# Expert stage of a two-layer decoder trunk: last strip's gate and up weights side by side, one-hot matrix transposed on another engine, activations' parts in the tokens' tile

## What is computed

```python
def swiglu(h, w_gate, w_up, w_down):
    return (jax.nn.silu(h @ w_gate) * (h @ w_up)) @ w_down

def moe_ffn(h, w_router, w_gate, w_up, w_down):       # hf: 256 x 1024
    logits = (hf @ w_router).astype(jnp.float32)
    top_vals, top_idx = lax.top_k(logits, TOP_K)      # TOP_K = 2 of 8
    top_w = jax.nn.softmax(top_vals, axis=-1)
    ...
    for e in range(N_EXPERTS):
        out = out + gates[:, e:e + 1].astype(hf.dtype) * swiglu(hf, w_gate[e], w_up[e], w_down[e])
```

## Time and profile before

| | |
|---|---|
| median of three runs | 1274.0 us (1270.16 to 1275.53) |
| profiled execution | 1273.91 us, span 1272.1 us |
| PE busy | 1231.5 us (97%) |
| DVE busy | 996.6 us (78%) |
| ACT busy | 831.1 us (65%) |
| POOL busy | 87.1 us (7%) |
| moved from and to HBM | 282 GB/s over the span |
| first expert item begins | about 485 us |
| last matmul of the last item begins | 1259.6 us |

### The profile page before, as it was taken

One profiled execution on the slowest core, in us unless ns is written; L12 is line 12 of the kernel. 1 busy time (PEld: TensorE's weight loads), 2 busy tenths in 40 slices (PEclk: granted clock), 3 DMA queues, 4 the chain that ended last, 5 costly groups with the idle time before them and its releaser, 6 DMA issues.

```text
span 1272.1 us, 17697 instructions
## 1 busy us (share of the span) xinstructions
PE 1231.5 (97%) x6322; PEld 1027.1 (81%) x6322; DVE 996.6 (78%) x1156; ACT 831.1 (65%) x919; POOL 87.1 (7%) x71
## 2 busy tenths in 40 slices
PE   8998999999999898999999999999999999999997
PEld 8976788888897576888888888888888888888775
DVE  4785566655668748898888888888888888888996
ACT  5556554454554746777777777777777777777764
POOL 2000000000000002010010010010010010010830
PEclk8988999999999899999999999999999999999999
DMA  9430665555452039999999999999999999999961
GB/s 295 153 132 2 205 226 178 188 175 193 121 182 101 16 105 398 394 387 375 392 366 369 391 363 362 392 366 375 391 363 369 392 362 370 392 364 369 396 224 50
DMA packets 186373, 357.54 MB, mean 281 GB/s; under 512 B 15255, under 2 KB 73173, under 8 KB 186292
## 3 DMA queue, kind: packets, MB, share of 16 engines
q1 hardware_dynamic: 183436, 344.89, 75.8%
q0 software_dynamic: 2688, 11.46, 2.4%
q10 hardware_dynamic: 200, 0.54, 0.1%
HBM read 351.11 MB, written 7.86 MB: 282 GB/s over the span
## 4 chain that ended last, share of the span: by engine, by line
PE 88%; DVE 6%; ACT 3%; issue 2%; DMA 1%; POOL 0%; SPq 0%; POOLq 0%; DVEq 0%; ACTq 0%
PE bank L1610 23%; PE bank L1612 23%; PE bank L1611 23%; PE bank L1911 6%; PE bank L1912 3%; PE bank L1979 1%; DVE lo_ring L1108 1%; PE bank L1689 1%; ACT hi_ring L766 1%; PE bank L1794 1%; DMA raw_a<-in_w_in 1%; DMA raw_a<-in_w_gate_dense 1%; PE bank L1960 1%; DVE lo_ring L1103 1%; DVE cv L1214 1%
## 5 line engine op out<-in xcount | busy, mean ns | idle before, releaser
L1108 DVE TENSOR_TENSOR lo_ring<-raw_m,hi_ring 128x2048 fp32r<-128x2048 f32 x168 | 389.6, 2328 | 53.4 <-ACT hi_ring L772 52.5
L772 ACT ACTIVATE hi_ring<-raw_m 128x2048 fp32r<-128x2048 f32 x168 | 322.2, 1918 | 80.0 <-PE bank L1612 80.0
L1610 PE MATMUL bank<-hi_ring,hT 128*128 128x512 f32 (+1 forms) x832 | 318.7, 383 | 3.2 <-DVE lo_ring L1108 3.0
L1612 PE MATMUL bank<-hi_ring,hT 128*128 128x512 f32 (+1 forms) x832 | 311.7, 375 | 0.0
L1611 PE MATMUL bank<-lo_ring,hT 128*128 128x512 f32 (+1 forms) x832 | 311.0, 374 | 0.0
L1108 DVE TENSOR_TENSOR lo_ring<-raw_a,hi_ring 128x2048 fp32r<-128x2048 f32 x96 | 220.8, 2310 | 35.9 <-ACT hi_ring L772 35.7
L772 ACT ACTIVATE hi_ring<-raw_a 128x2048 fp32r<-128x2048 f32 x96 | 183.4, 1920 | 53.5 <-PE bank L1612 52.3
L1610 PEld LDWEIGHTS bank<-hi_ring,hT 128*128 128x128 f32 x832 | 157.2, 189 | 33.7 <-DVE lo_ring L1108 6.9
L1103 DVE TENSOR_TENSOR lo_ring<-raw_a,hi_ring 128x2048 fp32r<-128x2048 f32 (+1 forms) x55 | 124.2, 2262 | 71.5 <-ACT hi_ring L766 71.4
L1612 PEld LDWEIGHTS bank<-hi_ring,hT 128*128 128x128 f32 x832 | 156.8, 188 | 28.8
L1611 PEld LDWEIGHTS bank<-lo_ring,hT 128*128 128x128 f32 x832 | 157.3, 189 | 26.4
(11 more groups left out here) (317 smaller groups left out, 1507.0 us busy)
## 6 DMA issues: line engine op xcount, KB each, us to landing
raw_m<-in_w_down_exp SPq DMA_DIRECT2D x80, 1024.0 KB, 7.0
raw_a<-in_w_up_exp SPq DMA_DIRECT2D x48, 1024.0 KB, 6.8
raw_m<-in_w_gate_exp SPq DMA_DIRECT2D x48, 1024.0 KB, 7.6
raw_a<-in_w_gate_exp SPq DMA_DIRECT2D x40, 1024.0 KB, 6.9
raw_m<-in_w_up_exp SPq DMA_DIRECT2D x40, 1024.0 KB, 7.9
raw_a<-in_w_in SPq DMA_DIRECT2D x12, 1024.0 KB, 6.4
raw_a<-in_w_gate_dense SPq DMA_DIRECT2D x11, 1024.0 KB, 5.4
raw_a<-in_w_up_dense SPq DMA_DIRECT2D x11, 1024.0 KB, 5.4
```

Of the source, the lines that this page charges most:

```text
L772: A(hi_of(NA + j), t, ACT.Copy).then_inc(hi_ready, 1)
L1108: V.tensor_tensor(lo_of(NA + j), expert_slot(i, j)[0], hi_of(NA + j).bitcast(F32), ALU.subtract).then_inc(lo_ready, 1)
L1610: M(o, lh, rh, start=start, stop=False)
L1612: return M(o, ll, rh, start=False, stop=stop)
```

## The change

Three things. (1) `m_hi` and `m_lo` are no tiles of their own any more but views of `y_hi` and `y_lo`, in the second half of `hT`. (2) The last strip's gate and up weights are put side by side: two pieces "GU", each with four blocks of 128 rows, 256 gate columns and 256 up columns, loaded by two transfers each. One matmul of 512 columns computes both into bank 0; Silu reads its left half and the product its right half. The list has 33 pieces as before and ends with GU, GU, D4, D4, D5. (3) TensorE's transposes of `onehot` and ScalarE's copies go. Instead VectorE keeps, per item, the slots' token numbers: the second column of the token table is raised by one, so that a slot without a token is told apart, and at U4 VectorE copies `tok_next` to `tok_now` and writes the next item's numbers from bank 7. After the last item it compares them with `iota` to make `onehot_t` once; `scatter` waits for that. VectorE's wait for the transposes ahead of `make_onehot` goes too.

```diff
@@ expert_order
     order = up("G", 0) + up("U", 0)
-    for c in range(1, EC):
+    for c in range(1, EC - 1):
         order += up("G", c) + up("U", c) + down(c - 1)
-    return order + down(EC - 1)
+    return order + [("GU", EC - 1, part) for part in range(2)] + down(EC - 2) + down(EC - 1)
@@ tables
-        one[:, K_TOK + 2 * t:K_TOK + 2 * t + 2] = (t * P + np.arange(P))[:, None]
+        one[:, K_TOK + 2 * t] = t * P + np.arange(P)
+        one[:, K_TOK + 2 * t + 1] = t * P + np.arange(P) + 1.0
@@ tiles
+        tok_now = sb("tok_now", [P, TT])
+        tok_next = sb("tok_next", [P, TT])
-        m_hi = sb("m_hi", [P, 2, 4, P], F32R)
-        m_lo = sb("m_lo", [P, 2, 4, P], F32R)
+        m_hi = y_hi.rearrange("p (c f s) -> p c f s", c=2, f=4)
+        m_lo = y_lo.rearrange("p (c f s) -> p c f s", c=2, f=4)
@@ helpers
+        def closes(kind, c, part, which):
+            return kind in (which, "GU") and last_part(kind, c, part)
+        def up_out(which, c):
+            if c < EC - 1:
+                return bank["GU".index(which)][:, 0:EW]
+            return bank[0][:, FC * "GU".index(which):FC * "GU".index(which) + FC]
         def transposed_after(kind, c, part):
-            if kind == "G" and c >= 1 and last_part(kind, c, part):
+            if kind == "G" and c >= 1 and last_part(kind, c, part) or kind == "GU" and part == 0:
                 return c - 1
@@ sync, expert_loads
+                    elif kind == "GU":
+                        rows = PIECE // EW * P
+                        for m, name in enumerate(("w_gate_exp", "w_up_exp")):
+                            src = a[name][0][one, part * rows:(part + 1) * rows, c * EW:c * EW + FC
+                                             ].rearrange("e (k p) n -> p (e k) n", p=P)
+                            sp.dma_start(expert_view(t, kind, c)[:, :, m * FC:(m + 1) * FC], src).then_inc(s, 16)
+                        continue
@@ scalar, item
-                    if kind == "G" and last_part(kind, c, part):
+                    if closes(kind, c, part, "G"):
                         act.wait_ge(piece_used, expert_done(i, "G", c))
                         act.wait_ge(prod_done, GU0 + c + i * EC)
-                        A(m_sg[:, 0:w], bank[0][:, 0:w], ACT.Silu).then_inc(sg_done, 1)
-                    if kind == "U" and c == 2 and part == 0:
-                        act.wait_ge(onehot_tmm, i + 1)
-                        A(onehot_t[:], bank[6][:, 0:TT * P].rearrange("p (t s) -> p t s", t=TT),
-                          ACT.Copy).then_inc(onehot_tdone, 1)
+                        A(m_sg[:, 0:w], up_out("G", c), ACT.Silu).then_inc(sg_done, 1)
@@ vector, item
-                    if kind == "U" and last_part(kind, c, part):
+                    if closes(kind, c, part, "U"):
-                        V.tensor_tensor(m_prod[:, 0:w], bank[1][:, 0:w], m_sg[:, 0:w], ALU.mult).then_inc(prod_done, 1)
+                        V.tensor_tensor(m_prod[:, 0:w], up_out("U", c), m_sg[:, 0:w], ALU.mult).then_inc(prod_done, 1)
                     if kind == "D" and c == 2 and part == 0:
-                        dve.wait_ge(onehot_tmm, i + 1)
+                        if first:
+                            dve.wait_ge(gather_mm, 4)
                     if kind == "U" and c == 4 and part == 0:
+                        if first:
+                            V.memset(tok_now[:], 0.0).then_inc(tok_moved, 1)
+                        else:
+                            dve.wait_ge(tok_kept, TT * i)
+                            V.tensor_copy(tok_now[:], tok_next[:]).then_inc(tok_moved, 1)
                         dve.wait_ge(slot_mm, i + 1)
                         V.tensor_copy(slot_i[:], bank[7][:, 0:1]).then_inc(slot_ready, 1)
+                        dve.wait_ge(tok_moved, i + 1)
+                        for t in range(TT):
+                            V.tensor_scalar(tok_next[:, t:t + 1], bank[7][:, 1:2], -1.0 - t * P, None, ALU.add
+                                            ).then_inc(tok_kept, 1)
@@ vector, after the last item
+            dve.wait_ge(tok_moved, n_items)
+            for t in range(TT):
+                V.tensor_scalar(onehot_t[:, t, :], iota, tok_now[:, t:t + 1], None, ALU.is_equal).then_inc(onehot_tdone, 1)
@@ tensor, scatter
+                    pe.wait_ge(onehot_tdone, TT)
@@ tensor, item
-                            pe.wait_ge(onehot_tdone, i + 1)
-                            if kind == "G":
+                            if kind != "U":
                                 pe.wait_ge(sg_done, GU0 + c + i * EC)
-                        o = bank[0 if kind == "G" else 1][:, 0:w]
-                        for kk in range(PIECE // w):
-                            k = part * (PIECE // w) + kk
+                        o = bank[1 if kind == "U" else 0][:]
+                        for kk in range(PIECE // EW):
+                            k = part * (PIECE // EW) + kk
-                    if kind == "U" and c == 2 and part == 0:
-                        for t in range(TT):
-                            r = nc.tensor.transpose(bank[6][:, t * P:(t + 1) * P], onehot[:, t, :].bitcast(F32), ident)
-                        r.then_inc(onehot_tmm, 1)
```

More of the change, by code:

```diff
@@ L445, in build @@
         gathered = sem("gathered")
-        onehot_tmm = sem("onehot_tmm")
+        tok_kept = sem("tok_kept")
+        tok_moved = sem("tok_moved")
         onehot_tdone = sem("onehot_tdone")
@@ L488, in expert_slot @@
             tile = raw_a[:, s, :] if s < RAW_A else raw_m[:, s - RAW_A, :]
-            return tile, raw_in[s], 16 * (trunk_uses[s] + j // RAW_M + 1) + i * (16 * NFF // RAW_M)
+            sent = [2 if E_ORDER[m % NFF][0] == "GU" else 1 for m in range(s, 2 * NFF, RAW_M)]
+            return tile, raw_in[s], 16 * (trunk_uses[s] + sum(sent[0:j // RAW_M + 1])) + i * (16 * sum(sent[0:NFF // RAW_M]))
         def in_piece_view(t, p):
@@ L514, in last_part @@
         def last_part(kind, c, part):
-            return part == expert_width(c) // FC - 1
+            return part == (2 if kind == "GU" else expert_width(c) // FC) - 1
         def expert_done(i, kind, c):
-            return NA + E_ORDER.index((kind, c, expert_width(c) // FC - 1)) + 1 + i * NFF
+            kind = "GU" if kind != "D" and c == EC - 1 else kind
+            parts = 2 if kind == "GU" else expert_width(c) // FC
+            return NA + E_ORDER.index((kind, c, parts - 1)) + 1 + i * NFF
         def expert_view(t, kind, c):
-            return t.rearrange("p (k n) -> p k n", n=D if kind == "D" else expert_width(c))
+            return t.rearrange("p (k n) -> p k n", n=D if kind == "D" else EW)
+        def closes(kind, c, part, which):
[4 more added lines that the diff above has]
+            return bank[0][:, FC * "GU".index(which):FC * "GU".index(which) + FC]
         def transposed_after(kind, c, part):
-            if kind == "G" and c >= 1 and last_part(kind, c, part):
+            if kind == "G" and c >= 1 and last_part(kind, c, part) or kind == "GU" and part == 0:
                 return c - 1
@@ L606, in expert_loads @@
                         src = a["w_down_exp"][0][one, f0:f0 + FC, :].rearrange("e (k p) n -> p (e k) n", p=P)
+                    elif kind == "GU":
[5 more added lines that the diff above has]
+                        continue
                     else:
                         w = a["w_gate_exp" if kind == "G" else "w_up_exp"][0]
-                        rows = PIECE // expert_width(c) * P
-                        src = w[one, part * rows:(part + 1) * rows, c * EW:c * EW + expert_width(c)
+                        rows = PIECE // EW * P
+                        src = w[one, part * rows:(part + 1) * rows, c * EW:(c + 1) * EW
                                 ].rearrange("e (k p) n -> p (e k) n", p=P)
@@ L1984, in item @@
                     pe.wait_ge(lo_ready, NR + j + 1 + i * NFF)
-                    w = expert_width(c)
                     wh, wl = expert_view(hi_of(NA + j), kind, c), expert_view(lo_of(NA + j), kind, c)
@@ L2017, in item @@
                     r.then_inc(piece_used, 1)
-                    if kind == "G" and c >= 1 and last_part(kind, c, part):
+                    if kind != "D" and transposed_after(kind, c, part) is not None:
                         transpose_act(i, c - 1)
```

## The result

The changed kernel takes 1261.46 us (median of five runs, 1260.95 to 1264.96) against 1273.9 us: a ratio of 0.9924, 95% interval 0.9909 to 0.994. On another chip the same kernel gave 0.990 (0.9879 to 0.9921). The profiled execution took 1263.28 us with a span of 1261.4, 10.6 us less than that of before. Forecast were 1269.9 us and 4.0 us less.

A forecast was written before the change was run, and what follows sets the result against it. TensorE was taken to bound the expert stage. Savings of 1.9 us (one-hot transposes) and 2.1 us (combined gate and up), the rest at zero, made 4.0 us off 1273.9: 1269.9 us, 8-in-10 range 1264.5 to 1275.0.

The forecast's parts named there:

- The bound: Expert stage: transfers wait for buffers, buffers for splits, splits for TensorE; a nanosecond off TensorE's stream is one off the kernel.
- Part 1, the one-hot matrix: Strip 2's up stage: dropping two TensorE transposes saves 0.27 us per expert, counted for seven experts, 1.9 us.
- VectorE's additions: Behind strip 4's first up split: 0.3 to 0.7 us per expert, taken as 0.4, hidden by 0.97 us slack, counted nothing.
- The final comparisons: Two VectorE comparisons at the end, about 0.48 us, fit into 4.19 us of idle time ahead of the final part.
- Part 2, gate and up side by side: Last strip: 24 wide matmuls replace 48 narrow ones, 5.91 us instead of 6.17, saving 0.26 per expert, 2.1 in all.
- rival a: Last strip: narrow matmuls cost exactly half of wide ones, so only the one-hot saving is left: 1272.0 us; chance 0.06.
- Part 3, order at the end of the strip: Last strip's Silu and product come later; slack before the product's transposes falls from 0.40 to about 0.25 us, cost nothing.
- Rival (d): Last strip's product comes too late for its transposes, by 1.66 us per expert: 1283.2 us, 0.7% slower; chance 0.04.
- (c): Transfers are the real bound, TensorE's savings become waits for data, time stays at 1273.9 us; chance 0.08.
- Part 3, the place: Down matmuls with m_hi and m_lo in the tokens' tile: counted zero, bounds -5.8 to +2.1 us over 1056 matmuls.
- Rival (b): The move into the tokens' tile makes down matmuls as quick as up ones: further 5.8 us, 1264.1 us; chance 0.10.

The follow-up runs named there:

- tile_only: The kernel before, with only m_hi and m_lo moved into the second half of the tokens' tile; 1266.7 us, ratio 0.9957.
- dense_too: The changed kernel with the dense layer's d_hi and d_lo moved over the tile xn at byte 106624; 1262.87 us, ratio 0.9919.

## Why the prediction was wrong

**The bound: right.** TensorE fills the middle experts before and after, and what its stages there saved is what the experts saved.

**Part 1, the one-hot matrix: right.** 0.27 us per expert expected, 0.30 measured. VectorE's additions in the changed kernel, timeline of DVE:

```profile
844.71 2.29 DVE L1128 TENSOR_TENSOR lo_ring<-raw_m,hi_ring 128x2048 fp32r<-128x2048 f32 x1 [1.11 <-ACT hi_ring L796]
846.91 0.16 DVE L1614 COPY tok_now<-tok_next 128x2 f32<-128x2 f32 x1
846.98 0.15 DVE L1616 CAST slot_i<-bank 128x1 uint32<-128x1 f32 x1
847.11 0.23 DVE L1619 TENSOR_SCALAR tok_next<-bank 128x1 f32<-128x1 f32 x2
847.25 2.31 DVE L1128 TENSOR_TENSOR lo_ring<-raw_m,hi_ring 128x2048 fp32r<-128x2048 f32 x1
```

Between the two splits lie 847.25 - 846.91 = 0.34 us, where the cast alone took 0.06 before: 0.28 us more, the lower end of my 0.3 to 0.7, and hidden as expected. The final comparisons (0.47 us from 1246.04) end 3.4 us before VectorE's next work. The last expert saved 1.0 us, about what the place (0.8) and the combined strip (0.24) explain, and so little or nothing from this part, as counted; in tile_only it saved 0.7.

**Part 2, gate and up side by side: right.** 5.91 us expected, 5.93 measured. Narrow matmuls at 0.120 us and wide ones at 0.227 (rival a falls); with the spacing of an isolated matmul that the Trainium skill gives ("TensorE: Matmul & The Clock Gate", Back-to-back issue gap) this part would have saved 0.06 us per expert by an estimate (24 times 2.5 ns, where the prediction says 2.7), and it saved 0.24.

**Part 3, order at the end of the strip: right.** The rows are the last product on VectorE and, above, the transposes of TensorE at 861.51:

```profile
858.65 2.29 DVE L1128 TENSOR_TENSOR lo_ring<-raw_m,hi_ring 128x2048 fp32r<-128x2048 f32 x1 [0.75 <-ACT hi_ring L796]
860.86 0.42 DVE L1583 TENSOR_TENSOR xn<-bank,xn 128x256 f32<-128x256 f32 x1
```

The product ends at 861.28, a slack of 0.23 us for the expected 0.25, and the transposes wait for nothing. Rival (d) falls. So does (c): the DMA engines moved 381 GB/s in a middle expert, SyncE's queue still waited 538.4 us for buffers, and the limit of 358 GB/s of the Trainium skill ("DMA: Bandwidth & Descriptors", Where 436 GB/s comes from) is again passed. That section of the Trainium skill gets it by halving a stack's bandwidth between two cores, and this kernel runs on one, so the figure may not apply here.

**Part 3, the place: wrong, and this is the step that failed.** I priced the move at nothing because the output projection, with weights in the tokens' tile, ran at "(145.95 - 134.86)/48 = 0.231 us". This mean has a stranger in it. These are the rows around its first matmul in the earlier trace rows, in the kernel before:

```profile
134.61 0.60 PE L1816 MATMUL bank<-xn,v_m 128*128 128x256 f32 x2
...
135.28 0.40 PE L1611 MATMUL bank<-lo_ring,hT 128*128 128x512 f32 x1
```

The stretch begins behind another kind of matmul, and its first step is 135.28 - 134.86 = 0.42 us. The other 47 take (145.95 - 135.28)/47 = 0.227 us. The row did not speak against the place, it agreed with it: weights in the tokens' tile, a bank that changes every three matmuls as in the down stage, and the spacing of the up stage. The up stage, under the same load of the other engines and the DMA, had 0.227 us too. Of what could make the down matmuls' 0.233, the address of m_hi and m_lo was left. The term that I put at zero measured 0.80 us per middle expert in tile_only (95.2 to 94.39), 132 matmuls of 0.006 us, and 5.7 us in the medians of that kernel and the one before beside it (1272.43 to 1266.7). Rival (b) was the right one. I had given it 0.10, and its price of 5.8 us was close: with the forecast's 4.0 it gives 1264.1, and the profiled execution took 1263.28. The median of the five runs is another 1.8 us lower than the profiled one. My range began at 1264.5, above my own price for (b).

**What stays open.** Why the weights' region matters to TensorE, and whether the height alone counts. The rings of the split weights, which are the moving operand, lie at bytes 16512 to 65664 in every kernel here, and none moved them. So "the weights lie high" and "the weights lie on the other side of the step than the moving operand" can't be told apart. Most of the raw buffers lie above the step too, but their traffic isn't needed for the effect: the dense layer loads only the low ones (`raw_a`), and its down matmuls were slow all the same. Open is also the start of the kernel. Of the time up to the first mark 1.4 us were saved, which is what one expert saves, but this term is not shown by itself. The first expert's first matmul starts at 491.98 us before, and at 490.44 and 491.96 in two profiles of the changed kernel; from there to the first mark it takes 89.65 us before, 89.82 and 88.49 after.

## What to carry to other kernels

Price a stream of equal instructions by the spacing between starts, and leave out the first step behind an interruption; if two stages of one engine with equal shapes differ in spacing, list what differs in their operands, addresses included, before calling it noise. Where TensorE is the bound, try the tiles that serve as its weights at other addresses, low ones first, and measure the whole stretch and not only the stage: in the experts this gave more than both edits that removed instructions, in the dense layer next to nothing. A rival that was given a price and a chance belongs inside the range.

## What the runs showed of the hardware

- With the moving operand at bytes 16512 to 65664, a 128x512 fp32r matmul is spaced 0.227 us when its weights and those of the next matmul lie below byte 138368 of a partition, and about 0.233 us (0.232 in the dense layer) when one of them lies at 142592 or above (178688 to 186880 and 203424 to 211616 measured too).
- Within the high region the exact byte counts a little: weights at 203520 take 94.65 us per expert, at 203488 94.82 to 94.85. Which property of the address it is, is open.
- The same gate and up matmuls of the dense layer take 11.29 or 11.10 us, in turn before and always 11.29 in dense_too, out of the same tiles at the same addresses.
- Alternating the output bank every three matmuls costs nothing: the down stage, with two banks, has the same 0.227 us as the up stage once its weights lie low.
- A duration in a row barely shows this: its median goes from 0.389 us with low weights to 0.395 or 0.397 with high ones, 0.39 or 0.40 in the rows. The starts show it.
